# A four-layer decoder trunk on one core: the eight idle products of the state-space layer are left out

## The reference

```python
def s5_mixer(x, w_in, a_re, a_im, log_dt, b_re, b_im, c_re, c_im, d_skip, w_glu, b_glu):
    u = x @ w_in                              # 64 groups x 16 channels
    ...                                       # lam, B, C from the parameters, zero-order hold
    def chunk_step(carry, uc):
        h0r, h0i = carry
        bur = jnp.einsum('gpc,blgc->blgp', bbr, uc)
        bui = jnp.einsum('gpc,blgc->blgp', bbi, uc)
        ...                                   # complex scan over positions, 64 states a group
        y = jnp.einsum('gcp,blgp->blgc', cr, hr) - jnp.einsum('gcp,blgp->blgc', ci, hi)
        return (hr[:, -1], hi[:, -1]), y
    ...
    y = y + d_skip.astype(f32) * u32.reshape(bsz, s, D_MODEL)
    y = jax.nn.gelu(y).astype(x.dtype)
    val, gate = jnp.split(y @ w_glu + b_glu, 2, axis=-1)
    return val * jax.nn.sigmoid(gate)
```

## Time and profile before

| | us |
|---|---|
| median of three runs | 1184.4 (1181.81 to 1185.47) |
| the profiled execution | 1182.76 |
| its span, first to last instruction | 1181.0 |
| TensorE busy | 1160.0 (98% of the span) |
| VectorE busy | 870.4 (74%) |
| ScalarE busy | 634.0 (54%) |
| granted TensorE clock, mean over the span | 0.996 of full |

### The profile page before, as it was taken

The page is one execution under the profiler, slowest core; times in us unless marked ns, Lnnn a source line. Parts: engine busy times, 40 slices in busy tenths (PEclk is TensorE's granted clock), DMA queues, the critical chain, the costliest instruction groups (busy, mean ns, idle before and its releaser), DMA issues.

```text
span 1181.0 us, 18769 instructions
## 1 busy us (share of the span) xinstructions
PE 1160.0 (98%) x7306; PEld 997.8 (84%) x7306; DVE 870.4 (74%) x1385; ACT 634.0 (54%) x1065; POOL 158.9 (13%) x212
## 2 busy tenths in 40 slices
PE   9999999999999999999999999999999999999996
PEld 7998799999977778888887888888878988888885
DVE  7789799989877687566667787666687768765665
ACT  6776354544545466455554556554538664655552
POOL 0640089102690000000000000000010000000000
PEclk9999999999999999999999999999999999999998
DMA  7675564655677558566664557656636434856650
GB/s 249 211 289 176 163 193 148 196 179 179 186 195 238 179 178 265 192 211 187 197 187 160 196 168 236 193 187 196 186 123 216 136 108 143 266 184 192 194 163 36
DMA packets 63968, 220.91 MB, mean 187 GB/s; under 512 B 8068, under 2 KB 9988, under 8 KB 63368
## 3 DMA queue, kind: packets, MB, share of 16 engines
q1 hardware_dynamic: 57224, 202.57, 53.8%
q0 software_dynamic: 5648, 15.73, 4.1%
q10 hardware_dynamic: 1008, 1.41, 0.4%
HBM read 211.03 MB, written 7.60 MB: 185 GB/s over the span
## 4 chain that ended last, share of the span: by engine, by line
PE 92%; DVE 4%; ACT 1%; issue 1%; DMA 1%; SPq 0%; DVEq 0%; ACTq 0%
PE bank L1636 19%; PE bank L1639 10%; PE bank L1651 9%; PE bank L1653 9%; PE bank L1657 9%; PE bank L1628 6%; PE bank L1629 6%; PE bank L1630 6%; PE bank L1760 5%; PE bank L1694 4%; PE bank L1949 1%; PE bank L1608 1%; PE bank L1795 1%; DMA raw<-in_w 1%; PE bank L1931 1%
## 5 line engine op out<-in xcount | busy, mean ns | idle before, releaser
L1015 DVE TENSOR_TENSOR wlo<-raw,whi 128x1024 fp32r<-128x1024 f32 x227 | 286.3, 1267 | 50.6 <-ACT whi L622 47.5
L622 ACT ACTIVATE whi<-raw 128x1024 fp32r<-128x1024 f32 x227 | 239.3, 1059 | 52.2 <-PE bank L1657 19.8
L1015 DVE TENSOR_TENSOR ext<-raw,ext 128x1024 fp32r<-128x1024 f32 x142 | 172.6, 1222 | 33.0 <-ACT ext L622 30.6
L1636 PE MATMUL bank<-xboth,whi 128*128 128x512 f32 x504 | 177.5, 394 | 0.0
L622 ACT ACTIVATE ext<-raw 128x1024 fp32r<-128x1024 f32 x142 | 149.2, 1060 | 22.5 <-DMA raw<-in_w 19.8
L1636 PE MATMUL bank<-xboth,ext 128*128 128x512 f32 x456 | 160.7, 394 | 0.6 <-ACT silu L703 0.6
L1639 PE MATMUL bank<-xboth,wlo 128*128 128x256 f32 x504 | 130.9, 280 | 0.0
L1628 PE MATMUL bank<-xboth,whi 128*128 128x256 f32 x432 | 122.7, 284 | 0.8 <-ACT qa_late L790 0.8
L1629 PE MATMUL bank<-xboth,whi 128*128 128x256 f32 x432 | 121.2, 281 | 0.0
L1630 PE MATMUL bank<-xboth,wlo 128*128 128x256 f32 x432 | 121.1, 280 | 0.0
L1639 PE MATMUL bank<-xboth,ext 128*128 128x256 f32 x456 | 118.5, 280 | 0.0
(11 more groups left out here) (399 smaller groups left out, 2377.7 us busy)
## 6 DMA issues: line engine op xcount, KB each, us to landing
raw<-in_w SPq DMA_DIRECT2D x370, 512.0 KB, 4.2
slot<-in_ln_row POOLq DMA_DIRECT2D x16, 512.0 KB, 5.5
toep<-slot POOLq DMA_DIRECT2D x8, 512.0 KB, 10.0
toepA<-toep SPq DMA_DIRECT2D x2, 1024.0 KB, 6.4
BT<-toep SPq DMA_DIRECT2D x2, 1024.0 KB, 6.4
x_tm<-in_x SPq DMA_DIRECT2D x2, 512.0 KB, 5.0
slot<-in_s_B SPq DMA_DIRECT2D x2, 512.0 KB, 4.7
slot<-in_s_C SPq DMA_DIRECT2D x2, 512.0 KB, 4.7
```

Source lines behind the costliest of these rows:

```text
L622: nc.scalar.activation(hi_of(c), raw[:, c % RAW, :], ACT.Copy).then_inc(w_hi, 1)
L1015: V.tensor_tensor(lo_of(c), raw[:, c % RAW, :], hi_of(c).bitcast(F32), ALU.subtract).then_inc(w_lo, 1)
L1636: return mm(dst[:, :], hi_of(c)[:, kc * P:(kc + 1) * P], xboth[:, kc, :, :].rearrange("p a t -> p (a t)"), start=kc == 0, stop=kc == KC - 1)
```

## The change

The four calls of `idle_products` in the S5 layer go, eight products in all. The call in the attention layers stays, and so does the function.

```diff
@@ s5(), the list of TensorE
                 u_turned(0)
                 u_turned(1)
-                idle_products(7, 256)
                 states_by_n(0)
                 states_by_n(1)
                 states(0)
...
                 states(1)
                 pe.wait_ge(u1_sb, 2)
                 swapped(1)
-                idle_products(7, 256, 3)
                 swapped_back(0)
-                idle_products(7, 256)
                 pe.wait_ge(ug0_sb, 2)
                 pe.wait_ge(ug1_sb, 2)
                 u_turned(2)
...
                 y_turned(0)
                 pe.wait_ge(g_sb, 3)
                 swapped(3)
-                idle_products(7, 256, 3)
                 pe.wait_ge(ylo_sb, 4)
                 glu(0, 0)
                 swapped_back(2)
```

## The result

The changed kernel took 1186.18 us (median of 20 runs, 1184.07 to 1188.92), the kernel before 1184.61 us (20 runs, 1181.47 to 1186.10). The medians differ by 1.57 us. The ratio on record is 1.0021, 95% interval 1.0014 to 1.0028, which stands for 2.5 us more, where 0.6 us less was forecast. The time lies within the stated range, but the sign was wrong. The profiled execution took 1185.73 us, with a span of 1183.9 us.

A forecast was written before the change was run, and what follows sets the result against it. TensorE, busy 1160.0 of 1181.0 us, was taken to bound the kernel. First product 0.63 us gained, other places 0, no clock fall: 1184.4 - 0.6 = 1183.8 us, 8 in 10 range 1181.2 to 1188.0.

The forecast's parts named there:

- the stated range: Whole kernel: 8 in 10 range for the time, 1181.2 to 1188.0 us.
- the sign: Whole kernel: forecast to get faster, 0.6 us less than the median of 1184.4 us.
- The first product, 0.63 us on the path: Product ahead of states_by_n(0): without it that stage and VectorE's L1496 start earlier, gain 0.63 us.
- Places 2, 3 and 4 are inside waits: Products ahead of and behind the first swapped_back and ahead of the first glu: they fill TensorE waits, gain 0.
- I take no fall, since each is shorter than both pauses that were followed by one: New S5-layer pauses of 1.75, 1.11 and 1.45 us: granted clock stays at 1.00, no cost in the sum.
- first rival (one or two falls): Pauses ahead of swapped_back(0) and glu: clock falls once or twice, 1185.3 or 1186.8 us; chance 0.28.
- second (low through the layer): Clock falls at about 365 us and stays low through the layer: 1188.4 us, upper end 1193; chance 0.12.
- That it costs something between 366 and 373 us at all: Fall behind the second place hits swapped_back(0) and u_turned(2), 1.11 us slack behind: cost 0 to 1.5 us.
- The rule of no pauses over about 3 us: Skill's rule for TensorE pauses: none of the new pauses matters, sum stands; prediction doubted it as a bound.

The follow-up runs named there:

- e2: Kernel before without only the three idle products ahead of the first swapped_back; ratio 1.0009, layer 23.94 us.
- e3: Kernel before without only the one idle product behind the first swapped_back; ratio 1.0007, layer 23.94 us.
- e4: Kernel before without only the three idle products ahead of the first glu; ratio 1.0022, layer 23.93 us.
- e8: The changed kernel once more, all eight products out, against the kernel before; ratio 1.0024, layer 25.91 us.
- e13: Kernel before without the three products ahead of the first swapped_back and the one behind it; ratio 1.0017, layer 26.58 us.
- e5: Kernel before without the first five idle products, keeping only the three ahead of the first glu; ratio 1.0033, layer 26.86 us.
- e6: Kernel before with only the three products ahead of the first swapped_back kept, the other five out; ratio 1.0008, layer 23.30 us.
- e9: Kernel before without the first product and the three ahead of the first swapped_back; ratio 0.9996, layer 23.31 us.
- e11: Kernel before without the first product and with two products instead of one behind the first swapped_back; ratio 1.0001, layer 23.32 us.
- e14: Kernel before without the first product and the three ahead of the first glu; ratio 1.0001, layer 23.31 us.
- e10: Kernel before without the first product, with twelve and four 128 x 128 transposes replacing the products ahead of and behind the first swapped_back; ratio 1.0002.

## Why the prediction was wrong

*The first product, 0.63 us on the path.* Right: L1496 came 0.63 us earlier in the changed kernel, and the layer was 0.61 to 0.63 us shorter in every profile with place 1 empty and the clock at full in it.

*Places 2, 3 and 4 are inside waits.* Right as far as TensorE's time goes: e2, e3 and e4 left the layer at 23.93 to 23.94 us. With the clock at full the pauses came out as 1.59, 1.02 (e3) and 1.31 us, 0.1 to 0.16 us shorter than worked out, since an idle time in the profile begins with the modelled end of the last matmul.

*"I take no fall, since each is shorter than both pauses that were followed by one."* This is the step that failed. The clock term of the sum was put at nothing, and the runs show 6.8 to 10.2 us at 1.2 GHz in its place, 2.4 to 3.6 us on the path. The half clock stands in the layer in all four profiles that have places 2 and 3 both empty (the changed kernel, e8, e13, e5), and in none of the thirteen others (e6 lost the clock at the layer's end, behind place 4). With one of the two filled, the mean clock was within 0.0004 of that of the kernel before (e2, e3, e9). The change removed the fillers from both.

The step had two faults. It weighed each pause by itself. And it took a single execution for what a pause always does. In the kernel before, the pauses of 0.80 and 1.02 us at the second LayerNorm left the clock at 1.00, and the prediction called that harmless; in five of the seventeen profiles (the changed kernel, e5, e9, e11, e14) the same two pauses were followed by 3.4 us at half clock. The long pause of the first LayerNorm, 2.43 to 3.00 us in the sixteen profiles where it isn't filled, was followed by such a stretch in only six of them. So no length of a pause parts those that lose the clock from those that don't, in these traces.

What it is about places 2 and 3 that loses the clock stays open. It is not that the second pause adds to the first: the fall came behind the start of the first L2068 by 2.27, 2.69, 2.85 and 0.11 us (the changed kernel, e8, e13, e5), before the second pause had begun. Nor does it take the second pause to keep the clock down: e5 had none, and the longest stretch. What stands ahead of the fall is the first pause of 1.59 us, one L2068 (only its start in e5) and, in three of the four, most of the small transposes. The product of place 3, where it is kept, stands just there, between L2068 and the transposes. A reading that fits is that too little full-sized work stood around the first pause; no run tests it.

The prediction's first rival (one or two falls) priced the place at up to 1.5 us, for one fall of 3.42 us; its second (low through the layer) had 4.6 us. What came lies between them. The two cases had 0.40 together.

*That it costs something between 366 and 373 us at all.* VectorE's work between the two scans hid what the transposes lost: the second L2068 starts 4.03 us behind the first, as in the kernel before (4.04). The loss came from `swapped_back(1)` and `states_by_n(2)`, 0.95 and 1.47 us, which the prediction had not named for a single fall.

*The rule of no pauses over about 3 us.* By the rule that the prediction took from the Trainium skill (TensorE: Matmul & The Clock Gate, section Why this matters for your kernels) the sum would have been left as it was. These traces don't agree with it as a guard: in e13 the pause ahead of the fall was 1.59 us, and at the second LayerNorm 1.02 us.

*The clock's share in the median.* Over the executions of e8 the mean granted clock is 0.9930 against 0.9965 for the kernel before on the same chip, which is 0.0035 x 1184 x 2 = 8 us more at half clock in each, about the length of the stretch in the profile. None of the changed kernel's 31 executions is above 0.995, and 87 of the other's 119 are. So the stretch is there in most executions, not in a few. Of the 2.5 us of the result, the layer's 1.8 to 2.0 us are shown by two profiles; the rest is within the interval and the open question of place 4.

## What to carry to other kernels

A matmul into a wait can be worth its place by the clock alone. Before taking filler out, mark every pause that it leaves, and weigh those that stand a few microseconds apart together, with the small instructions between them. Don't call a pause harmless because the clock held behind it in one profile: profile the same kernel several times, or read the mean clock over many executions. The price of a fall is what stands on the path while the clock is low, here two stages further on than the pause. To hold the clock it was enough to fill one of the two places, and a filler that delays the next engine's input (place 1) can go.

## What the runs showed of the hardware that was not expected

- With places 2 and 3 both empty, 6.8 to 10.2 us at 1.2 GHz began 0.1 to 2.9 us behind the restart from a pause of 1.59 us, in four profiles of four; the same pause with the product of place 3 behind it was not followed by a fall in two of two (e2, e9).
- The same pauses in the same code did not give the same clock: behind 0.80 and 1.02 us at the second LayerNorm it fell in 5 of 17 profiles, behind 2.43 to 3.00 us at the first in 6 of 16.
- The clock did not come back after 3.4 us as it had at 132.76 us in the kernel before. In e5 it stayed at 1.2 GHz for 10.2 us in which TensorE shows no idle time.
- At places 2 and 3, transposes of 128 x 128 held the clock as well as products do (e10: ratio 1.0002, interval 0.9991 to 1.0013).
- The 64 records of L2045's small products took 3.64 us at 1.2 GHz (e13) and 1.95 at 2.4 GHz, so they follow the clock by a factor of 1.9 in spite of their size.
- ScalarE's wait for a weight tile at about 885 us scattered from 5.93 to 7.73 us over the seventeen profiles of nearly the same program, and TensorE's wait behind it from 0.3 to 2.1 us.
